# Retention's rotary step moved from GpSimd to VectorE, behind the scaled keys of the recurrence

## What is computed

```python
def rotary(x, positions):
    ...
    x1, x2 = x32[..., :half], x32[..., half:]
    return jnp.concatenate([x1 * cos - x2 * sin, x1 * sin + x2 * cos], axis=-1)

def retention(q, k, v, positions, ret_norm_g):
    ...
    qh = rotary(q.reshape(B, T, H, dh), positions)
    kh = rotary(k.reshape(B, T, H, dh), positions) * (dh ** -0.5)
    ...
    scores = jnp.einsum('bhnid,bhnjd->bhnij', qc, kc) * decay_mask[None, :, None]
```

## Time and profile before

| | us |
|---|---|
| median of 3 runs | 1578.39 |
| lowest, highest | 1576.77, 1582.22 |
| the profiled execution, its own time | 1582.88 |
| its span, first instruction to last | 1581.0 |
| TensorE busy | 1538.2 (97%) |
| VectorE busy | 1005.7 (64%) |
| ScalarE busy | 712.1 (45%) |
| GpSimd busy | 563.0 (36%) |

### The profile page before, as it was taken

One profiled execution on the slowest core, in us unless ns is written; L12 is line 12 of the kernel. 1 busy time (PEld: TensorE's weight loads), 2 busy tenths in 40 slices (PEclk: granted clock), 3 DMA queues, 4 the chain that ended last, 5 costly groups with the idle time before them and its releaser, 6 DMA issues.

```text
span 1581.0 us, 35399 instructions
## 1 busy us (share of the span) xinstructions
PE 1538.2 (97%) x15704; PEld 1414.6 (89%) x15704; DVE 1005.7 (64%) x1637; ACT 712.1 (45%) x1126; POOL 563.0 (36%) x452
## 2 busy tenths in 40 slices
PE   9999999999999999999999999999999999999998
PEld 8989987899978989987999989999998899999887
DVE  4364386878784445576777786766446777764356
ACT  4554534544445455435444444633332555433223
POOL 3745613000217745503000310734673006446640
PEclk9999999999999999999999999999999999999999
DMA  9433364787545423474676545453333354533332
GB/s 357 169 122 108 113 232 191 265 299 273 187 166 211 161 89 125 161 279 187 250 283 240 204 142 182 152 176 133 135 136 135 124 197 153 182 133 138 114 130 93
DMA packets 43944, 281.49 MB, mean 178 GB/s; under 512 B 5144, under 2 KB 5272, under 8 KB 14352
## 3 DMA queue, kind: packets, MB, share of 16 engines
q1 hardware_dynamic: 42192, 270.13, 47.4%
q0 software_dynamic: 1600, 9.10, 1.5%
HBM read 278.15 MB, written 1.06 MB: 177 GB/s over the span
## 4 chain that ended last, share of the span: by engine, by line
PE 78%; DVE 13%; ACT 3%; issue 3%; POOL 2%; DMA 0%; POOLq 0%; SPq 0%; ACTq 0%; DVEq 0%
PE ps L613 75%; DVE part0l L1453 3%; DVE part1l L1453 3%; PE ps L621 3%; ACT part0h L2523 1%; DVE rows L1890 1%; ACT part1h L2523 1%; DVE Pr L1887 1%; ACT gates L2520 1%; ACT Xh L2523 1%; DVE Xl L1468 1%; DVE small L1484 0%; DMA ring<-in_w 0%; DVE raw L2012 0%; DVE mgx L2144 0%
## 5 line engine op out<-in xcount | busy, mean ns | idle before, releaser
L2523 ACT ACTIVATE part1h<-ring 128x1024 fp32r<-128x1024 f32 (+1 forms) x216 | 215.8, 1047 | 226.0 <-PE ps L613 213.6
L2523 ACT ACTIVATE part0h<-ring 128x1024 fp32r<-128x1024 f32 (+1 forms) x216 | 213.0, 1035 | 209.6 <-PE ps L613 194.3
L613 PE MATMUL ps<-Xh,part1h 128*128 128x256 f32 x968 | 276.7, 286 | 7.5 <-DVE Xl L1468 2.4
L613 PE MATMUL ps<-Xh,part0h 128*128 128x256 f32 (+1 forms) x952 | 270.9, 285 | 3.4 <-DVE Xl L1468 1.3
L613 PE MATMUL ps<-Xl,part1h 128*128 128x256 f32 x968 | 271.1, 280 | 0.0
L613 PE MATMUL ps<-Xh,part1l 128*128 128x256 f32 x968 | 270.9, 280 | 0.0
L613 PE MATMUL ps<-Xl,part0h 128*128 128x256 f32 (+1 forms) x952 | 265.2, 279 | 0.0
L613 PE MATMUL ps<-Xh,part0l 128*128 128x256 f32 (+1 forms) x952 | 265.1, 278 | 0.0
L3020 POOL TENSOR_TENSOR part1l<-ring,part1h 128x512 fp32r<-128x512 f32 x144 | 185.3, 1317 | 102.5 <-ACT part1h L2523 102.3
L3020 POOL TENSOR_TENSOR part0l<-ring,part0h 128x512 fp32r<-128x512 f32 x144 | 185.3, 1318 | 101.8 <-ACT part0h L2523 101.7
L1453 DVE TENSOR_TENSOR part1l<-ring,part1h 128x1024 fp32r<-128x1024 f32 (+1 forms) x144 | 181.3, 1299 | 52.3 <-ACT part1h L2523 52.0
(11 more groups left out here) (446 smaller groups left out, 3260.4 us busy)
## 6 DMA issues: line engine op xcount, KB each, us to landing
ring<-in_w SPq DMA_DIRECT2D x211, 1024.0 KB, 4.9
hid<-in_ada SPq DMA_DIRECT2D x36, 512.0 KB, 6.3
hid<-in_w SPq DMA_DIRECT2D x6, 1024.0 KB, 11.1
rows<-in_lnrow POOLq DMA_DIRECT2D x6, 1024.0 KB, 9.9
fqk<-in_ada SPq DMA_DIRECT2D x6, 512.0 KB, 6.1
cq<-in_ada SPq DMA_DIRECT2D x6, 512.0 KB, 6.5
gates<-in_c SPq DMA_DIRECT2D x2, 1536.0 KB, 9.5
ring<-in_w SPq DMA_DIRECT2D x4, 512.0 KB, 5.6
```

What stands on the lines that cost most here:

```text
L613: return e.matmul(o, a, b, start=st, stop=sp)
L2523: return e.activation(o, a, ACT.Copy)
```

## The change

`rotate` leaves GpSimd's program and stands in VectorE's, called in `prepare` directly behind L2263, the second of the scaled keys. The two products with the cosines and with the sines are each one operation over all 512 columns instead of two over 256; sums and differences stay at 256 columns. So per layer 24 GpSimd operations become 16 of VectorE. The signal `rot` now comes from VectorE. Nothing else is different.

```diff
@@ vector_program
+    def rotate(l):
+        Z = M.Z[l]
+        a, b = (M.grow[:, 512 * k:512 * k + 512] for k in range(2))
+        a8, b8 = (t.rearrange("p (x d) -> p x d", d=64) for t in (a, b))
+        a4, b4 = (v(t, h=4, s=2, d=64) for t in (a, b))
+        w.wait_ge(*at["cs"])
+        for src, n in ((Z.rq3, "rq"), (Z.rk3, "rk")):
+            w.wait_ge(*at[n + "0", l])
+            w.wait_ge(*at[n + "1", l])
+            for i in range(2):
+                s8 = src[:, i, :].rearrange("p (x d) -> p x d", d=64)
+                s4 = src[:, i, :].rearrange("p (h s d) -> p h s d", h=4, s=2)
+                w.wait_ge(*V.now())
+                for t8, cs in ((a8, 0), (b8, 1)):
+                    e.tensor_tensor(t8, s8, M.cs[:, cs, i, :].unsqueeze(1).to_broadcast([128, 8, 64]), ALU.mult).then_inc(*V())
+                w.wait_ge(*V.now())
+                e.tensor_tensor(s4[:, :, 0, :], a4[:, :, 0, :], b4[:, :, 1, :], ALU.subtract).then_inc(*V())
+                e.tensor_tensor(s4[:, :, 1, :], b4[:, :, 0, :], a4[:, :, 1, :], ALU.add).then_inc(*V("rot", l))
...
         e.tensor_tensor(kt, k4, ee, ALU.mult).then_inc(*V("k", l))
+        rotate(l)
         jobs.fill()
@@ gpsimd_program
-    def rotate(l):
...
     def job2(l, name):
         if "." in name:
             use_half(l, name)
         else:
             use(l, name)
-        if name == "rk1":
-            rotate(l)
```

## The result

The changed kernel takes 1586.89 us (median of 5 runs, 1586.54 to 1589.19), the kernel before 1578.56 us beside it (5 runs): ratio 1.0053, 95% interval 1.0041 to 1.0065. It is 8.3 us slower. The forecast was 1584.9 us, range 1579.5 to 1589.5. The profiled execution took 1589.19 us.

A forecast was written before the change was run, and what follows sets the result against it. TensorE, busy 97%, bounds the kernel, but VectorE holds the chain while GpSimd rotates. Later rg0 starts net of savings (+3.1 us) plus lost clock (+3.4) make +6.5: 1584.9 us against the 1578.39 median, range 1579.5 to 1589.5.

The forecast's parts named there:

- VectorE's operations shorten without GpSimd: VectorE from 1005.7 us to the scaled keys: 7.2 us less work per layer; low halves 1.22 us instead of 1.75.
- the half in flight when the rotation began: VectorE's low half already running at 1005.7 us: its remainder gives 0.3 us of the 7.2 us less work.
- Rival 3: Something else makes VectorE's rows long, so moving the rotation frees nothing: rg0 8.2 us later per layer, 1596.9 us; chance 0.07.
- 6.1 of the 7.2 us arrive: At the scaled keys (L2263): of 7.2 us less VectorE work, 6.1 arrive, so keys are done near 1026.0 us.
- rival 2: Keys early enough (rv0's low half starting 3 us earlier), so TensorE's holes go: gains 4.5 and 3.6 us, 1570.3; chance 0.08.
- The rotation, 8.7 us: 16 added VectorE operations behind the keys, ahead of rg0's low half: 8.7 us per layer, bounds 7.4 and 11.7.
- rg0 starts 2.2 us later: TensorE's rg0 product waits for its low half behind the rotation: starts at 1036.15 us against 1033.96.
- One idle time of 5.6 us: TensorE between the turns (1030.5 us) and rg0 (1036.15): one gap of some 5.6 us instead of four holes.
- What rg0 gets back inside, 1.1 and 0.25 us: Inside rg0 on TensorE: hitches go in both layers, 0.83 us of issue in layer 0; 1.1 and 0.25 us back.
- The loads at nothing: Constants' load starts 5 us earlier, pg1's load 2 us later; nobody waits for either, so both cost nothing.
- The clock, 1.7 us per layer: TensorE behind the gap before rg0: one 3.4 us stretch at 1.2 GHz costs 1.7 us per layer, 3.4 together.
- Rival 1: Order ahead of rg0 costs its 3.1 us, but the clock holds or returns in the gap: 1581.5 us; chance 0.30.

The follow-up runs named there:

- experiments 5 to 7: Kernel before with no rotation; at its place GpSimd does 36 memsets (1578.05 us), 31 memsets (1573.08 us) or 41 copies behind one memset (1598.53 us) per layer.
- experiment 2: Changed kernel plus ten unread TensorE matmuls between the turns of the keys and rg0: 1579.39 us, ratio 1.0004 to the kernel before.
- experiment 1: Changed kernel with the rotation one place later on VectorE, behind rg0's low half: 1573.75 us, ratio 0.9968 to the kernel before.
- experiment 9: Changed kernel with three quarters of the rotation ahead of rg0's low half and the last quarter behind: 1581.21 us, ratio 1.0013 to the kernel before.
- experiment 4: Changed kernel with its products cut into halves of 256 columns, 24 operations per layer for 16: 1588.78 us, ratio 1.0063 to the kernel before.

## Why the prediction was right, point by point

The sign, the mechanism and the range held; the sum was 1.8 us short (6.5 against the 8.3 of the medians), 2.8 short against the stretch itself (9.26). It was not saved by errors that cancel: the clock (2.1 short), rg0's start (0.5) and what rg0 gets back (0.2) all erred to the same side, and the range was wide enough for them.

- **VectorE's operations shorten without GpSimd: held.** L1453 is at 1.22 us, the 128x4 operations at 0.17. The cause was read rightly in the earlier trace rows, and experiments 5 to 7 narrow it to reading. One small part did not come: the half in flight when the rotation began (0.3 us in the prediction) is the one of 3.37 us, which is stretched by the modified keys and not by the rotation. Rival 3 (the change frees nothing) is out.
- **"6.1 of the 7.2 us arrive", keys done near 1026.0: 1026.85.** The waits that I set came, in the right places: VectorE stood 1.4 us before rv0's low half, for ScalarE. But that half started at 1014.45 and not 1013.7. u0 itself started no earlier: the hole before it is still 0.23 us (I had most of it gone), since the low half that ends it is that same one of 3.36 us. The prediction had u0 end near 1012.0 and ScalarE follow; as u0 ended no earlier, ScalarE's copy began at 1012.88 (1012.75 before), and copy and half took 1.57 us. So rival 2, which wanted this start 3 us earlier, is out too, by the point that it named.
- **The rotation, 8.7 us: 8.45.** A tile takes 2.12 us (1026.88 to 1029.00), where I had 2.18: the waits cost less than the 0.06 I gave each. The 7.4 us that the Trainium skill's figure gave (VectorE: DVE Perf Modes, the TRN2 errata) is 1.05 too low, and the section itself says that this row under-predicts the duration of a single operation; the rows of the same size were the better price.
- **rg0 starts 2.2 us later: 2.47** in both layers, counted from u0 (2.65 in layer 0 by the times of the two traces, as u0 itself starts 0.18 later in the second).
- **One idle time of 5.6 us: 4.77.** TensorE ended the turns at 1031.84, where I had 1030.5. Of these 1.3 us, 0.7 is the hole before u0, 0.4 what came back behind u0's start less than I had (1.9 for 2.3; the slower spacing of the matmuls, below), and 0.2 the later u0. It cost nothing: rg0's start is set by VectorE.
- **What rg0 gets back inside, 1.1 and 0.25 us: 0.90 and 0.25** (9.22 and 8.46 us before, 8.32 and 8.21 in experiment 2). The 0.83 us of issue is indeed gone when TensorE waits ahead of rg0, and comes back at 1.01 us in experiment 1, where it does not.
- **The loads at nothing: held.** SyncE's queue issues the constants' load at 1024.28 us, 4.5 earlier, and the piece behind rg0 at 1037.63, 2.1 later; nobody waits for either.
- **The clock, 1.7 us per layer: 2.8 and 2.7. This is the term that was mis-sized.** I took one stretch like that of the earlier trace rows, 1.7 us, and kept 3.4 per layer only as a bound. Behind 4.8 us the low level lasted 6 us into rg0, not 3.4. The Trainium skill's warning (TensorE: Matmul & The Clock Gate, Why this matters for your kernels) is borne out by experiments 1 and 2, which take the idle time away in two ways and both keep the clock at 1.00.

With the measured terms: 2 x 2.47 for the start, 1.15 back inside rg0, 5.47 for the clock: 4.94 - 1.15 + 5.47 = 9.26 us. Rival 1 (the clock holds, 1581.5) is what experiment 2 built, and it came to 1579.4.

What the prediction did not look for is that the gain it had worked out was there to be taken. It wrote that the removal "gains through VectorE" and that 6.1 us arrive at the keys, and then asked only what stands behind them. The low half needs none of the rotation's results, and nobody needs the rotation before TensorE's transposes. In experiment 1 the rotation ends at 1037.26 us and the transposes begin at 1041.01: 3.7 us of slack on that side, too.

## What to carry to other kernels

When work is moved onto an engine that feeds the bound, ask for each operation behind it in the queue who waits for it, and put the moved work behind the ones that are waited for: the change with these 16 operations costs 8.3 us or gains 5.0, by which side of one low half they stand on. Before waits of TensorE are gathered into one, count what the clock costs behind it: here 5.5 us beside 3.8 of later start. And before an engine is freed of work because its neighbour is slow, look at what it does to shared memory: here GpSimd's clears cost VectorE nothing and its copies a third.

## What the runs showed of the hardware that was not expected

**The clock does not fall at a sharp length of idle time.** The changed kernel kept it behind 1.92 us near 1546 and lost it behind 1.93 us near 1222, the same place of the other layer; the kernel before lost it behind 1.94, and experiment 9 did both behind 2.65. The kernel before even lost it behind 1.42 us put down to issue:

```profile
1481.02 0.46 PE L613 MATMUL ps<-cg,bkN 64*64 64x64 f32 x17 [1.42 <-issue]
...
1481.00:1484.00 3.00, 2.98 (x34) 2.91 (x34) 0.00 (x0) 0.00 (x0) 0.14 (x1) 0.61 0.57 180
```

(its timeline of TensorE, and the stretch from there). Behind 4.8 us and more it was lost each time, with 6 us of work at the low level in the changed kernel.

**TensorE's matmuls go at one of two spacings at the full clock.** The 128x256 matmuls stand 0.113 or 0.118 us apart; each restart behind a wait settles on one, and in the stretches read here, u0 to the turns, a run without waits keeps it. The same 48 matmuls of u0 in layer 1, in the chain of the changed kernel:

```profile
1331.47 5.91 PE ps L613 x48
```

and in that of experiment 4, whose instructions for TensorE are the same:

```profile
1331.03 5.72 PE ps L613 x48
```

Over the four pieces up to the turns this is 24.90 against 24.07 us, 0.83 us that no wait explains. In the changed kernel all of this stretch goes at the slower spacing, where before each wait gave a new start, mostly at the faster one. Closing the holes so gave back 1.9 us behind u0's start (26.80 to 24.89), where I had 2.3 (0.9 and 1.4). In experiment 1 the turns end 24.9 us behind u0's start in both layers, so the slower spacing is also a part of why it stayed above 1571. What chooses the spacing is open.

**One operand read on GpSimd stretches a two-input operation of VectorE** from 1.22 to 1.63 us, the two of the rotation's products to 1.75, and clears, which read nothing, not at all. I had expected that only two inputs on both sides collide. How far two operands stretch it depends on the GpSimd operation: beside the product of 128x1024 it took 3.36 us (shown with the result), that is 2.1 us more than alone, while that product took 2.39. What decides between 1.75 and 3.36 no run shows.
